# The expert stage of a two-block transformer kernel: the three steps of a pair of experts in one stretch, gathers and scatters behind them

## What is computed

```
g_prob = softmax(xf @ w_rg)            # 4 groups of 8 experts, best group per token
e_w, e_i = top_k(softmax(e_logits of that group), 2)
weights = g_gate * e_w / sum(e_w)
hdn = silu(xb @ w1[e]) * (xb @ w3[e])  # xb: the tokens of expert e, 1024 -> 512
ys  = hdn @ w2[e]                      # 512 -> 1024
out[token] += ys * weight
```

## Time and profile before

| | |
|---|---|
| three runs | 1589.33, 1589.94, 1591.72 us |
| span of the profiled execution | 1591.2 us |
| time of that execution around the span | not shown apart; the span lies inside the three runs |
| PE busy | 1536.0 us, 97% |
| DVE busy | 718.0 us, 45% |
| ACT busy | 531.0 us, 33% |
| transfers of expert weights (M<-in_w) | 192 of 1024 KB |

### The profile page before, as it was taken

The page is one execution under the profiler, slowest core; times in us unless marked ns, Lnnn a source line. Parts: engine busy times, 40 slices in busy tenths (PEclk is TensorE's granted clock), DMA queues, the critical chain, the costliest instruction groups (busy, mean ns, idle before and its releaser), DMA issues.

```text
span 1591.2 us, 19637 instructions
## 1 busy us (share of the span) xinstructions
PE 1536.0 (97%) x7802; PEld 1080.1 (68%) x7802; DVE 718.0 (45%) x1208; ACT 531.0 (33%) x910; POOL 164.3 (10%) x172
## 2 busy tenths in 40 slices
PE   6899999999999999999999999999999999999998
PEld 5666688889888888888777777745444444444366
DVE  5335423455444444468665787532132132132174
ACT  5234422344332423345355577331011011010042
POOL 1013200002111111111300210011000000000000
PEclk9999999999999999999999999999999999999999
DMA  7111332213222222222110232779999999999961
GB/s 272 54 53 60 141 111 96 103 57 116 106 106 81 105 84 102 106 93 83 54 50 27 94 119 77 296 287 384 422 421 421 417 420 421 419 420 421 421 247 54
DMA packets 45437, 311.22 MB, mean 196 GB/s; under 512 B 5136, under 2 KB 5648, under 8 KB 10016
## 3 DMA queue, kind: packets, MB, share of 16 engines
q1 hardware_dynamic: 42336, 296.22, 46.8%
q0 software_dynamic: 3008, 13.72, 2.4%
HBM read 301.52 MB, written 8.39 MB: 195 GB/s over the span
## 4 chain that ended last, share of the span: by engine, by line
PE 89%; DVE 3%; DMA 3%; ACT 2%; issue 2%; DVEq 0%; ACTq 0%; POOLq 0%
PE bank L788 21%; PE bank L2461 13%; PE bank L832 8%; PE bank L1389 6%; PE bank L2477 6%; PE bank L841 6%; PE bank L2494 4%; PE bank L2444 4%; PE bank L2660 3%; PE bank L1246 3%; DMA M<-in_w 3%; PE bank L801 2%; PE bank L858 1%; PE bank L849 1%; PE bank L1987 1%
## 5 line engine op out<-in xcount | busy, mean ns | idle before, releaser
L612 DVE TENSOR_TENSOR w_lo<-M,w_hi 128x2048 fp32r<-128x2048 f32 x73 | 168.8, 2317 | 180.2 <-ACT w_hi L607 180.2
L2461 PE MATMUL bank<-M 128*64 128x512 f32 x1024 | 227.4, 595 | 2.9 <-DMA M<-in_w 2.9
L607 ACT ACTIVATE w_hi<-M 128x2048 fp32r<-128x2048 f32 x73 | 139.0, 1911 | 148.4 <-PE bank L788 56.9
L788 PE MATMUL bank<-HTH,w_hi 128*128 128x512 f32 x432 | 168.1, 389 | 0.0
L788 PE MATMUL bank<-HTL,w_hi 128*128 128x512 f32 x432 | 168.1, 389 | 0.0
L788 PE MATMUL bank<-HTH,w_lo 128*128 128x512 f32 x432 | 168.1, 389 | 0.0
L2461 PEld LDWEIGHTS bank<-M 128*64 128x64 f32 x1024 | 71.2, 137 | 138.7 <-issue 137.6
L2477 PE MATMUL bank<-M 128*64 128x512 f32 x512 | 114.0, 596 | 3.0 <-DMA M<-in_w 2.8
L2619 DVE TENSOR_TENSOR X<-bank,X 128x512 f32<-128x512 f32 x69 | 46.6, 689 | 112.4 <-PE bank L2494 112.3
L788 PEld LDWEIGHTS bank<-HTH,w_hi 128*128 128x128 f32 x432 | 81.1, 188 | 16.9
L788 PEld LDWEIGHTS bank<-HTH,w_lo 128*128 128x128 f32 x432 | 81.1, 188 | 16.8
(11 more groups left out here) (365 smaller groups left out, 2876.4 us busy)
## 6 DMA issues: line engine op xcount, KB each, us to landing
M<-in_w SPq DMA_DIRECT2D x192, 1024.0 KB, 9.7
M<-in_wd SPq DMA_DIRECT2D x78, 1024.0 KB, 4.8
M<-in_nb SPq DMA_DIRECT2D x4, 1536.0 KB, 6.5
X<-in_x SPq DMA_DIRECT2D x4, 512.0 KB, 7.8
M<-in_rows POOLq DMA_DIRECT2D x4, 512.0 KB, 5.4
M<-in_tb POOLq DMA_DIRECT2D x8, 256.0 KB, 4.0
rowb<-in_rows POOLq DMA_DIRECT2D x4, 512.0 KB, 5.5
xs_parts<-XSH POOLq DMA_DIRECT2D x1, 2048.0 KB, 10.8
```

The lines of the kernel that those rows point to most:

```text
L607: e.activation(hi[:, :], slots[slot_of[n]], ACT.Copy).then_inc(split_hi_done, 1)
L612: e.tensor_tensor(lo[:, :], slots[slot_of[n]], hi[:, :], ALU.subtract).then_inc(split_lo_done, 1)
L788: m = e.matmul(out[:, :], w[:, k0 + k, n0:n0 + 128], v[k], start=(k == 0 and i == 0), stop=(k == len(hi) - 1 and i == 2))
L2461: m = e.matmul(b[64 * s:64 * s + 64, :], Xe[:, 4 * kh + k, o + C * s:o + C * s + C], unit_w(key, 4)[:, k, :], start=(kh == 0 and k == 0), ...
```

## The change

The list of the expert stage is put in another order; nothing else is changed. A helper `all_steps(p)` gives the three steps of a stretch with nothing between them. In the stretch of an even pair the four gather pieces of the next group and then `tu` follow; in that of an odd pair all eight scatter pieces of the group before, then `gs`, `tu`. In pair 0 the two `pl` pieces follow the two steps instead of standing behind one each, in pair 1 all four gather pieces stand behind the steps. Ahead of the last step stood three pieces of group 6 and five of pair 14; now the eight pieces of group 6 stand in the stretch of pair 15, and the five of pair 14 stay. The numbers of instructions, the transfers and their order are the same.

```diff
+        def all_steps(p):
+            return steps_of(p, 0) + steps_of(p, 1) + steps_of(p, 2)
+
         for i in range(NPAIR // 2):
             p, g = 2 * i, i + 1
-            def gather(*kps):
-                return [("gx", g, kp) for kp in kps if g < NPAIR // 2]
+            gathers = [("gx", g, kp) for kp in range(4) if g < NPAIR // 2]
             turned = [("gs", 2 * g), ("gs", 2 * g + 1)] if g < NPAIR // 2 else []
             nxt = [("one_hot", g + 1)] if g + 1 < NPAIR // 2 else []
             if i == 0:
-                MOE += steps_of(0, 0) + [("pl", 3, 0)] + steps_of(0, 1) + [("pl", 3, 1), ("gs", 0), ("gs", 1), ("one_hot", 1), ("tu", 0)]
-                MOE += steps_of(1, 0) + gather(0) + steps_of(1, 1) + gather(1) + steps_of(1, 2) + gather(2, 3) + turned
-                MOE += [("tu", 1)] + nxt
+                MOE += all_steps(0) + [("pl", 3, 0), ("pl", 3, 1), ("gs", 0), ("gs", 1), ("one_hot", 1), ("tu", 0)]
+                MOE += all_steps(1) + gathers + turned + [("tu", 1)] + nxt
                 continue
-            MOE += steps_of(p, 0) + gather(0) + scatter(i - 2, 5) + steps_of(p, 1) + scatter(i - 2, 6, 7)
-            MOE += steps_of(p, 2) + gather(1) + [("tu", p)]
-            MOE += steps_of(p + 1, 0) + scatter(i - 1, 0, 1) + gather(2) + steps_of(p + 1, 1) + gather(3) + scatter(i - 1, 2)
-            MOE += steps_of(p + 1, 2) + scatter(i - 1, 3, 4) + turned + [("tu", p + 1)] + nxt
-        MOE += scatter(6, 5, 6, 7) + scatter(7, *range(5)) + steps_of(NPAIR, 2) + [("sc0", n // 2, n % 2) for n in LEFT] + scatter(8, *range(8))
+            MOE += all_steps(p) + gathers + [("tu", p)]
+            MOE += all_steps(p + 1) + scatter(i - 1, *range(8)) + turned + [("tu", p + 1)] + nxt
+        MOE += scatter(7, *range(5)) + steps_of(NPAIR, 2) + [("sc0", n // 2, n % 2) for n in LEFT] + scatter(8, *range(8))
```

## The result

Four runs of the changed kernel took 1609.84 to 1616.70 us, median 1613.16; the kernel before beside them 1588.64 to 1591.72, median 1589.63. The ratio is 1.0134, 95% interval 1.0119 to 1.0149: slower by 21 us (19 to 24); the two medians lie 23.5 apart. Forecast were 1608, that is 18.4 us more, and a range of 1596 to 1630.

A forecast was written before the change was run, and what follows sets the result against it. The prediction took the expert stage to be bound by the weight stream and PE together. Twelve pairs losing 15.7 us and 2.7 us at the end made 18.4, added to 1589.9 for 1608 us; range 1596 to 1630.

The forecast's parts named there:

- The bound: Expert stage: weight stream (60.0 us per group) and PE (60.08) both at their limit; changed kernel held by the stream.
- PE gains 0.9 us per group and gets nothing for it: Expert stage: PE's work per group falls from 60.08 to 59.2 us, but the DMA still needs 60.0.
- The round: Last half-step of one pair to the next, pairs 2 to 13: 25.7 + L against 30.0, losing 1.3 us per pair.
- The light stretches: PE's gathers or scatters with turns behind a pair's steps, nothing read meanwhile: 8.27 or 8.77 us.
- L: Time from issue to landing of a weight transfer with no queue ahead: taken at 5.6 us, ends 4.7 and 7.6.
- The start: Pairs 0 and 1: buffers come free sooner, the gather block gives it back; zero, ends 4.2 us gain, 1 us loss.
- The end: Pair 15: three more scatter pieces of group 6 behind the last wait make the last step 2.7 us later.
- The sum: Whole kernel: 15.7 us for twelve pairs plus 2.7 at the last step, 18.4 us slower, 1608 us.
- The queue carrying the swing: Rival, expert stage: the queue covers the light work, no loss per pair, only 2.7 us remain, 1593 us; chance 0.08.
- The early release: Rival, pairs 0 and 1: stream at full pace up to 4.2 us earlier and keeps it, 1588 us; chance 0.05.
- The clock: Rival, expert stage: twelve new PE waits each cost 1.7 us more through clock falls, 1628 us; chance 0.12.
- Long restarts: Rival, expert stage: every restart has L at 7.1 to 7.6 us, giving 1626 to 1632 us; chance 0.11.

The follow-up runs named there:

- the half-byte runs: Half the bytes in each expert-weight transfer behind the first twelve: kernel before 1584.2 us (ratio 0.9959), changed kernel 1572.0 (0.9883).
- The ring of six: Six weight buffers instead of seven: kernel before 1603.9 us (ratio 1.0088), changed kernel 1643.5 (1.0327).
- the two places: Changed kernel with each stretch's light work split, half behind the second step, half behind the third (pair 15 unsplit): 1593.8 us, ratio 1.0013.
- the block per group: Changed kernel with all gather and scatter pieces of a group in one block behind the odd pair: 1654.4 us, ratio 1.0392.
- the run with early start and end: Kernel before with pairs 0 and 1 in the changed order and group 6's eight scatter pieces ahead of pair 15's third step: 1587.9 us, ratio 0.9983.
- the early end alone: Kernel before with all eight scatter pieces of group 6 ahead of the third step in pair 15's stretch: 1589.0 us, ratio 0.9984.
- 2.4 alone: Kernel before with all eight scatter pieces of group 6 behind the third step in pair 15's stretch: 1594.1 us, ratio 1.0015.
- the pieces moved all the way: Changed kernel with all eight scatter pieces of group 6 ahead of the third step in pair 15: 1607.2 us, ratio 1.0099.
- the quarter run: Changed kernel with one of four gather and two of eight scatter pieces moved ahead of the third step (pair 15 unchanged): 1597.9 us, ratio 1.0035.

## Why the prediction was right

The time lies 3 to 5 us over the forecast of 18.4 more, well inside the range, and the mechanism is the one forecast; the sizes of several terms were off and partly cancelled.

**The bound.** Right. The changed kernel is held by the stream, the kernel before by the stream and PE about equally, and the half-byte runs show it from the other side: the same change without the stream as a bound is a gain.

**PE gains 0.9 us per group and gets nothing for it.** The second half is right, the size was not: 1.43 us per group. The sum took 7.02 us for every step; behind another step it is 6.87 to 6.94. It did not touch the forecast, as PE's saving is not on the path.

**The round.** Right in form. The ring of six (+2.5 us per pair), the two places (loss gone) and the block per group (a loss nearly three times as large) each change one term of it, and the time follows. The light stretches came out at 8.30 and 8.79 for 8.27 and 8.77, and a loss of 1.55 us per round was measured for 1.3 (12 x 1.3 is 15.6, where the sum has 15.7).

**L.** Taken at 5.6, measured 5.2 in the mean of twelve restarts. With 5.2 alone the loss would be 0.9. The trace gives the terms of the round, in the mean of the twelve: 15.97 us from the start of the last half-step to the restart (15.54 forecast), L 5.23, 10.21 for the four landings behind (10.0 forecast), and the 0.14. The first is longer by 0.3 because each of its two half-steps releases its buffers 3.63 or 3.65 us behind its start and not 3.51, and by 0.14 because the clock fell in one round. The four landings took 9.9 to 10.0 us in eight rounds and 10.6 to 10.9 in the other four (last section). So L was 0.4 too long and the rest 0.6 too short; that the sum came out within 0.3 is in part luck. Nor was L that of an empty queue: where the transfer ahead landed 2.8 to 3.1 us behind the restart, L was 5.3 to 5.9, where it landed 1.0 to 2.0 behind, 4.7 to 5.3, and in the one restart with nothing under way 4.9. The Trainium skill (DMA: Bandwidth & Descriptors, Anatomy of one DMA) gives an estimated 4.4 us for such a transfer by its formula for GpSimd's path; no restart here, on SP's, was under 4.7. The Trainium skill's page Perfetto Trace Analysis (Optimization Strategy) says that the same gap coming back can mean too few buffers; this trace agrees: the gap comes once per pair, and one buffer less makes it longer by 2.4 us, about one transfer.

**The start.** Forecast as zero between -4.2 and +1, because the gathers behind pair 1 would give the lead back at once. They did not: against the stage's start the last half-step of pair 1 comes 3.5 us earlier and that of pair 2 still 2.4. Whether the lead lasts is not settled. In the run with early start and end the last transfer of the stage lands 470.5 us behind the first up step, as in the kernel before, and its time does not differ from that of the early end alone. One reading was wrong beside this: pair 1 does not wait for its landings in the kernel before; the first wait of that stage is the one at 1123.13, in pair 2.

**The end.** 2.7 forecast, 2.7 in the trace, 2.4 alone, and some 6 with the pieces moved all the way, which the intervals alone don't settle.

**The sum.** Forecast were 15.7 for the rounds, 2.7 for the end and nothing for the start. The profiled spans have 19.6 for the twelve rounds, 0.9 for the one behind them, 2.7 for the end and a gain of 2.4 at the start. The loss of the rounds came out a quarter larger than forecast, and the start made up for part of it.

**The rivals.** The queue carrying the swing is refuted by the share of 0.98 and by the restarts. The early release does not decide: its gain was there, 2.4 us up to pair 2, but the rounds cost eight times as much. The clock did fall, but once in the profiled stage, behind the longest wait but one, and it cost the 1.7 us that was put on it (5.33 for a half-step of 3.65):

```profile
1155.48 5.33 PE L2475 MATMUL bank<-M 128*64 128x512 f32 x16 [2.04 <-DMA M<-in_w]
```

Between 1155 and 1161 us the granted clock is 0.72, that is the lower of the two levels for a part of it; the other waits of the stage left it at 1.00, the longest (2.27 us, at 1408.51) among them. Long restarts of 7 us did not come in these twelve; what made the two long ones in the earlier trace rows no run shows.

## What to carry to other kernels

When a stream of weights and the compute both run at their limit, the order of the work between them is part of the transfer plan: the half-step ahead of the light work, the light work, the half-step behind it and the time from an issue to its landing must together fit into the ring's stream and one transfer more, here 8 x 2.50 = 20.0 us. With an L of 5.2 they were 20.7 in the changed kernel and 18.9 in the quarter run, and the latter still lost some 3 us, so leave a margin. Work the round out (last release, light stretch, first release, landing) before grouping; grouping may well save the engine time, as it did here, and lose more on the stream. Work that needs no transfer belongs where the engine waits for the last ones, not behind them.

## What was not expected of the hardware

A stream whose queue is short moves less even while its engines count as busy. In the changed kernel the first issue behind the light stretch at 1139.1 us came before the queue was empty. Two windows of 2 us, there and behind the restart at 1204.8, and one further on:

```profile
1139.80:1141.80 2.00, 2.00 (x12) 0.65 (x10) 0.00 (x0) 0.00 (x0) 0.00 (x0) 1.00 0.91 246
...
1205.30:1207.30 2.00, 2.00 (x12) 0.72 (x10) 0.00 (x0) 0.00 (x0) 0.00 (x0) 1.00 0.71 217
1209.00:1219.00 10.00, 9.57 (x46) 2.99 (x40) 0.69 (x1) 0.00 (x0) 0.00 (x0) 1.00 1.01 424
```

At a share of 0.91 the full stream would move some 380 GB/s; it moved 246. So a restart costs more than the idle time that the share shows. In the kernel before with six buffers there is hardly any idle time at all, and the same dips:

```profile
1349.00:1353.00 4.00, 4.00 (x23) 1.88 (x20) 0.00 (x0) 0.60 (x1) 1.86 (x4) 1.00 1.00 348
```

The landings say when: between 1120 and 1480 us, 13 of 140 came more than 2.75 us behind the one before, against 2 of 145 with seven buffers. Eleven of the 13 were transfers issued with only two others under way, which held for 30 of the 140. Beyond 2.49 us each the 13 cost 10.9 us. That is most of the +14 us where the round allows for 3.5, and it would explain the 3 us left in the quarter run. What in the engines takes this time no run here shows; that the depth of the queue decides it is argued from the runs with six and seven buffers and from these landings.
